# The rest of each weight slab made on VectorE, in a float32 transformer pair of blocks

## The reference, cut to what matters

```python
# block 1
proj = rmsnorm(x, attn_norm_g) @ w_in            # 1024 x 2312
x = x + concat(window_attention, forgetting_attention) @ w_out
x = x + square(relu(rmsnorm(x, mlp_norm_g) @ w_up)) @ w_down     # 1024 -> 4096 -> 1024
# block 2; the six mod vectors are silu(c) @ w_mod + b_mod (1024 x 6144)
h  = rmsnorm(x, g_pre_mix) * (1 + scale) + shift
x = x + gate * rmsnorm(concat(pool_mixer, neighbourhood_attention) @ w_out_2, g_post_mix)
x = x + gate2 * rmsnorm(square(relu(h2 @ w_mlp_in)) @ w_mlp_out, g_post_mlp)
```

## Time and profile before

| | us |
|---|---|
| three timed runs | 1270.38, 1274.62, 1275.14; median 1274.62 |
| the profiled execution, its own time | 1270.3 |
| its span, first to last instruction | 1268.4 |
| TensorE busy | 1208.7 (95%) |
| VectorE busy | 610.9 (48%) |
| ScalarE busy | 464.6 (37%) |
| GpSimd busy | 450.8 (36%) |

### The profile page before, as it was taken

The page is one execution under the profiler, slowest core; times in us unless marked ns, Lnnn a source line. Parts: engine busy times, 40 slices in busy tenths (PEclk is TensorE's granted clock), DMA queues, the critical chain, the costliest instruction groups (busy, mean ns, idle before and its releaser), DMA issues.

```text
span 1268.4 us, 16854 instructions
## 1 busy us (share of the span) xinstructions
PE 1208.7 (95%) x6252; PEld 998.0 (79%) x6252; DVE 610.9 (48%) x907; ACT 464.6 (37%) x828; POOL 450.8 (36%) x188
## 2 busy tenths in 40 slices
PE   5799999998999999999899999999899999999997
PEld 4677877787788788788779887778788888888885
DVE  5555445658767768651657223884721111111115
ACT  5455433425324334234342111432463251341441
POOL 3422220204444453463336320400255435353440
PEclk9999999999999999999889999999999999999999
DMA  7422120206665766643424311202243324233211
GB/s 228 116 85 67 62 87 2 85 17 216 233 215 191 241 211 210 227 134 132 133 67 143 99 67 26 67 2 83 67 140 108 119 67 132 67 105 94 83 50 66
DMA packets 75562, 144.10 MB, mean 114 GB/s; under 512 B 7234, under 2 KB 10050, under 8 KB 75490
## 3 DMA queue, kind: packets, MB, share of 16 engines
q1 hardware_dynamic: 53730, 98.46, 24.7%
q10 hardware_dynamic: 21760, 44.67, 10.6%
HBM read 140.20 MB, written 2.13 MB: 112 GB/s over the span
## 4 chain that ended last, share of the span: by engine, by line
PE 54%; issue 22%; DVE 11%; POOL 8%; ACT 2%; DMA 1%; ACTq 0%; POOLq 0%; DVEq 0%
PE gemm L950 16%; PE gemm L952 16%; PE gemm L951 16%; POOL w_lo L513 8%; DVE nmax L1860 1%; PE aux L1404 1%; DVE prob_t L1674 1%; DVE gemm L1859 1%; PE aux L991 1%; DVE xr L1465 1%; DVE xr L1460 1%; ACT junk L576 1%; DVE xt_lo L1471 1%; DMA mlp_gain<-in_g_pre_mlp 1%; PE gemm L1088 1%
## 5 line engine op out<-in xcount | busy, mean ns | idle before, releaser
L513 POOL TENSOR_TENSOR w_lo<-w_raw,w_hi 128x1024 fp32r<-128x1024 f32 (+1 forms) x180 | 445.7, 2498 | 780.2 <-ACT w_hi L741 422.3
L950 PE MATMUL gemm<-xt_hi,w_hi 128*128 128x512 f32 (+1 forms) x704 | 255.9, 363 | 5.0 <-issue 4.6
L951 PE MATMUL gemm<-xt_lo,w_hi 128*128 128x512 f32 (+1 forms) x704 | 254.8, 362 | 0.0
L952 PE MATMUL gemm<-xt_hi,w_lo 128*128 128x512 f32 (+1 forms) x704 | 254.5, 362 | 0.0
L950 PE MATMUL gemm<-w_hi,ht_hi 128*128 128x512 f32 x512 | 201.4, 393 | 3.8 <-POOL w_lo L513 3.8
L951 PE MATMUL gemm<-w_lo,ht_hi 128*128 128x512 f32 x512 | 200.0, 391 | 0.0
L952 PE MATMUL gemm<-w_hi,ht_lo 128*128 128x512 f32 x512 | 199.7, 390 | 0.0
L741 ACT ACTIVATE w_hi<-w_raw 128x1024 fp32r<-128x1024 f32 x124 | 125.7, 1050 | 175.6 <-PE gemm L952 130.0
L950 PEld LDWEIGHTS gemm<-xt_hi,w_hi 128*128 128x128 f32 x704 | 134.0, 190 | 27.1 <-issue 6.0
L1699 DVE TENSOR_TENSOR ht_lo<-hid,ht_hi 128x512 fp32r<-128x512 f32 x64 | 53.0, 828 | 210.7 <-ACT hid L754 210.7
L951 PEld LDWEIGHTS gemm<-xt_lo,w_hi 128*128 128x128 f32 x704 | 133.9, 190 | 20.2
(11 more groups left out here) (218 smaller groups left out, 1487.0 us busy)
## 6 DMA issues: line engine op xcount, KB each, us to landing
wm<-in_w_mod ACTq DMA_DIRECT2D x64, 512.0 KB, 4.8
w_raw<-in_w_in SPq DMA_DIRECT2D x32, 512.0 KB, 3.8
w_raw<-in_w_up SPq DMA_DIRECT2D x32, 512.0 KB, 4.0
w_raw<-in_w_down SPq DMA_DIRECT2D x32, 512.0 KB, 4.1
w_raw<-in_w_mlp_in SPq DMA_DIRECT2D x32, 512.0 KB, 4.2
w_raw<-in_w_mlp_out SPq DMA_DIRECT2D x32, 512.0 KB, 3.7
w_raw<-in_w_out SPq DMA_DIRECT2D x16, 512.0 KB, 3.7
x<-in_x SPq DMA_DIRECT2D x4, 512.0 KB, 7.7
```

The lines of the kernel that those rows point to most:

```text
L513: pool.tensor_tensor(w_lo[s % 2][:, ks, 0:width], raw[q][:, :, 0:width], w_hi[s % 2][:, ks, 0:width].bitcast(F32), ALU.subtract).then_inc( ...
L950: pe.matmul(bank, lh, rh, start=(k == 0), stop=False)
L951: pe.matmul(bank, lh, rl, start=False, stop=False)
L952: mm = pe.matmul(bank, ll, rh, start=False, stop=(k == KT - 1))
```

## The change

GpSimd no longer makes any w_lo; it keeps the four subtractions of the pooled rows. VectorE gets `low(s, q)`, the same subtraction on the same shapes with the same two semaphores, called at places written out by hand:

- slab 0: two units after the `scaled` of token tiles 1 and 2 of norm 1;
- slabs 1 and 2: two units ahead of `head_means(g)` for g = 0, 1 and 4, 5;
- slabs 3 to 7: one unit at the end of the half that follows the one in which ScalarE rounded it;
- both MLPs: of the next slab all four units at c = 0, of the one after two units each at c = 4 and 5, and of the two that follow (the second down slab and the next chunk's first up slab) one or two units each at c = 8, 9, 10, 12, 13 and 14;
- block 2: four units in a row after the last chunk, after the pool mixer's tiles, after the q tiles and after the k_c tiles; the second slab of w_out_2 one unit each in steps 5, 7, 9 and 11 of the neighbourhood attention; and four units ahead of tile 6 of w_out_2.

On ScalarE one thing moves: the units 4 to 7 of a chunk are rounded two at a time, before the ReLUs of tiles 4 and 5, where they were one each before tiles 4 to 7.

```diff
--- before.py
+++ after.py
@@ -64,7 +64,7 @@
 TILE_MLP2 = TILE_OUT2 + 2 * TT
 
 OUT2_ORDER = ((0, 0), (1, 0), (0, 1), (1, 1), (0, 2), (0, 3), (1, 2), (1, 3))
-POOL_SPLIT_IN = (13, 15, 17, 19)
+POOL_SPLIT_IN = (13,)
 SPLIT_IN_ATTENTION = (4, 6, 8, 10)
 
 
@@ -506,34 +506,10 @@
 
         @block_fn(nc, ctx, "gpsimd")
         def _(pool):
-            def low(s, q, width, wait):
-
-                pool.wait_ge(hi_split, wait)
-                ks = slice(UK * q, UK * (q + 1))
-                pool.tensor_tensor(w_lo[s % 2][:, ks, 0:width], raw[q][:, :, 0:width],
-                                   w_hi[s % 2][:, ks, 0:width].bitcast(F32), ALU.subtract).then_inc(unit_split, 1)
-
-            def lows(first, slabs):
-
-                with pool.Fori(0, slabs // 2) as i:
-                    for a in range(2):
-                        for q in range(UQ):
-                            low(first + a, q, NC, i * 8 + (4 * (first + a) + q + 1))
-                if slabs % 2:
-                    for q in range(UQ):
-                        low(first + slabs - 1, q, NC, 4 * (first + slabs - 1) + q + 1)
-
-            for s in range(N_IN1 + 1):
-                for q in range(UQ):
-                    low(s, q, KV_W if s == 1 else NC, 4 * s + q + 1)
-            lows(SLAB_OUT1 + 1, SLAB_OUT2 - SLAB_OUT1)
-            for q in range(UQ):
-                low(SLAB_OUT2 + 1, q, NC, 4 * (SLAB_OUT2 + 1) + q + 1)
             pool.wait_ge(pool_hi, 1)
             for j in range(4):
                 pool.tensor_tensor(xt_lo[:, j, :], pooled[:, j, :], xt_hi[:, j, :].bitcast(F32),
                                    ALU.subtract).then_inc(pool_lo, 1)
-            lows(SLAB_MLP2, SLABS - SLAB_MLP2)
 
 
         @block_fn(nc, ctx, "scalar")
@@ -757,8 +733,9 @@
                     for c in range(4):
                         split(c, i)
                     for c in range(8):
-                        if c >= 4:
-                            split(c, i)
+                        if c in (4, 5):
+                            split(2 * c - 4, i)
+                            split(2 * c - 3, i)
                         squared_relu(c, i)
                         if mod:
                             modulation(16 * i + c)
@@ -1473,10 +1450,21 @@
                                           token_cols(hi, half, cols, permute).bitcast(F32), ALU.subtract), xt_lo_done)
 
 
+            def low(s, q, i=0):
+
+                width = KV_W if s == 1 else NC
+                ks = slice(UK * q, UK * (q + 1))
+                dve.wait_ge(hi_split, i * 16 + (4 * s + q + 1))
+                dve.tensor_tensor(w_lo[s % 2][:, ks, 0:width], raw[q][:, :, 0:width],
+                                  w_hi[s % 2][:, ks, 0:width].bitcast(F32), ALU.subtract).then_inc(unit_split, 1)
+
             dve.wait_ge(gain1_loaded, 16)
             for m in range(TT):
                 stat(STAT_N1 + m)
                 scaled(NT_1 + m, STAT_N1 + m, x[:, m, :], gain1[:])
+                if m in (1, 2):
+                    low(0, 2 * m - 2)
+                    low(0, 2 * m - 1)
                 if m:
                     xt_low(NT_1 + m - 1, m - 1)
             xt_low(NT_1 + 3, 3)
@@ -1538,6 +1526,9 @@
                                           hst[:, 3, :].unsqueeze(2).broadcast_to([P, NH, HD]), ALU.mult), gemm_free)
 
             for g in range(PHASE):
+                if g % 4 < 2:
+                    low(g // 4 + 1, 2 * (g % 4))
+                    low(g // 4 + 1, 2 * (g % 4) + 1)
                 head_means(g)
                 head_rows(g)
 
@@ -1662,6 +1653,8 @@
                     xt_low(NT_2 + m, m, halves=[half])
                 for kind, n in halves_of(MIX_TURN, h):
                     mix_low(kind, n)
+                if h - 1 in SPLIT1:
+                    low(*SPLIT1[h - 1])
 
             mean_square(STAT_N2 + 3, STAT_N2 + 4)
             norm2_rows(3)
@@ -1685,13 +1678,20 @@
                                       aux[2 + b % 2][:].rearrange("p (h d) -> p h d", d=HD),
                                       rden[:, cols].unsqueeze(2).broadcast_to([P, NH, HD]), ALU.mult), heads_out)
 
-            def mlp(t0, acc, up0, mod, after, fresh=False):
+            def mlp(s0, t0, acc, up0, mod, after, fresh=False):
 
                 f0 = freed(t0 - 1)
 
                 def chunk(i, mod, after, fresh=False):
+
+                    def lows(*cs):
+                        for e in cs:
+                            if not isinstance(i, int) or 4 * i + s0 + e // 4 + 1 < SLABS:
+                                low(s0 + e // 4 + 1, e % 4, i)
+
                     for c in range(16):
                         bank = gp[(t0 + c) % 4]
+                        lows(*{0: (0, 1, 2, 3), 4: (4, 5), 5: (6, 7), 8: (8,), 12: (12,)}.get(c, ()))
                         if c < 8:
 
                             dve.wait_ge(hid_hi, i * 8 + (up0 + c + 1))
@@ -1707,6 +1707,8 @@
                                 dve.tensor_copy(cols, bank[:]).then_inc(gemm_free, 1)
                             else:
                                 dve.tensor_tensor(cols, cols, bank[:], ALU.add).then_inc(gemm_free, 1)
+                            if c % 4 < 3:
+                                lows(c + 1)
                             if after is not None:
                                 dve.wait_ge(gemm_free, i * 8 + (f0 + c - 7))
                                 after(c)
@@ -1791,7 +1793,9 @@
 
             did(dve.tensor_copy(ctmp[:, 0, :], csil[:, 0, :]), wm_used)
             modulation(-1)
-            mlp(TILE_MLP1, x, 0, True, norms_of_block_2)
+            mlp(SLAB_MLP1, TILE_MLP1, x, 0, True, norms_of_block_2)
+            for q in range(UQ):
+                low(SLAB_IN2 + 1, q)
             xt_low(NT_3 + 3, 3, True)
 
 
@@ -1817,10 +1821,14 @@
                                              upad[:, 8:8 + S], ALU.mult, ALU.subtract), pool_done)
                 g += 1
             assert tally.n[pool_step.name] == POOL_STEPS
+            for q in range(UQ):
+                low(SLAB_IN2 + 2, q)
             for j in range(4):
                 dve.wait_ge(gemm_done, g + 1)
                 did(dve.tensor_scalar(q_2[:, j, :], gp[g % 4][:], QSCALE, None, ALU.mult), gemm_free)
                 g += 1
+            for q in range(UQ):
+                low(SLAB_IN2 + 3, q)
             for j in range(4):
                 dve.wait_ge(gemm_done, g + 1)
                 did(dve.tensor_copy(k_2[:, j, :], gp[g % 4][:]), gemm_free)
@@ -1829,6 +1837,8 @@
                 dve.wait_ge(gemm_done, g + 1)
                 did(dve.tensor_copy(k_c[:, j, :], gp[g % 4][:, 0:CTX]), gemm_free)
                 g += 1
+            for q in range(UQ):
+                low(SLAB_OUT2, q)
             for j in range(4):
                 dve.wait_ge(pool_mixed, j + 1)
                 did(dve.tensor_scalar(pooled[:, j, :], aux[j][:], pscale[:, j:j + 1], None, ALU.mult), pool_scaled)
@@ -1872,6 +1882,8 @@
                         dve.wait_ge(turn_hi, 2 * TT + k + 1)
                         did(dve.tensor_tensor(grid_cols(xt_lo, k), grid_bank(aux[w % 2]),
                                               grid_cols(xt_hi, k).bitcast(F32), ALU.subtract), turn_read)
+                if i - 1 in SPLIT_IN_ATTENTION:
+                    low(SLAB_OUT2 + 1, SPLIT_IN_ATTENTION.index(i - 1))
 
 
             dve.wait_ge(tail_loaded, 16 * 5)
@@ -1884,6 +1896,9 @@
                 cols = slice(j * NC, (j + 1) * NC)
                 if e == 5:
                     xt_low(NT_4, 0)
+                if e == 6:
+                    for q in range(UQ):
+                        low(SLAB_MLP2, q)
                 dve.wait_ge(gemm_done, g + 1)
 
                 dve.wait_ge(ssq_done, tail_squares(e))
@@ -1922,7 +1937,7 @@
                     did(dve.scalar_tensor_tensor(x[:, m, cols], sub[:, m, cols], st[:, 3, k:k + 1], x[:, m, cols],
                                                  ALU.mult, ALU.add), fin_step)
 
-            mlp(TILE_MLP2, sub, 8 * NCH, False, last_norm, fresh=True)
+            mlp(SLAB_MLP2, TILE_MLP2, sub, 8 * NCH, False, last_norm, fresh=True)
 
 
 SILU_STEPS = 3 + 5 + 4
```

## The result

The changed kernel took 1267.49 us (median of four runs, 1266.03 to 1267.79), the kernel before in the same session 1274.63 (1270.38 to 1275.14). The ratio is 0.9941, with a 95% interval of 0.9923 to 0.9960: a gain of 7.1 us, where 17.3 were forecast.

What follows compares the result with a forecast made beforehand. TensorE was taken as the bound, busy 1208.7 of 1268.4 us, with waits on GpSimd's w_lo and on VectorE standing still behind GpSimd. Stage terms summed to -17.3, from the median 1274.6 to 1257.3 us; range 1247 to 1272.

Steps and rivals of the forecast that it cites:

- its own signs of being wrong: Mod steps over 1 us, new TensorE waits over 1 us for hid_lo, a maximum or w_lo, or changed full-clock busy time.
- Opening, heads (0 and -1.5): 0 to 66 us: opening unchanged; in the heads TensorE's waits for qn shrink, -0.8 for the first, -0.7 for two others.
- First attention (+1): 20 subtractions, 24.6 us of VectorE, placed between maxima and copies, hardly delay TensorE: +1, bounds 0 and 24.6.
- Start of the first MLP (-5.2): Mod steps finish sooner, the 3.6 us wait for mod_lo goes, and 1.6 us of clock returns: -5.2.
- Rest of the first MLP (-3.8): Three waits for w_lo at c = 8 go because the slab's fourth unit is finished by tile 6: -3.8.
- Norms of block 2 (-8): Waits shrink by 3.2 and 2.1, the clock returns 4.2, a late xt_lo costs 1.5: -8, bounds -2 and -10.
- w_out_2 and second MLP (-2.4): A 2.5 us wait behind VectorE's standstills goes; the second MLP has nothing to give: -2.4.
- Neighbourhood attention (+2.6): Four subtractions in the loop of VectorE and TensorE each cost 0.64 us beyond idle time: +2.6, bounds 0 and 5.
- The level: The profiled execution took 1270.3 us; the forecast sum was instead set on the runs' median, 1274.6 us.
- the gain comes in part: Rival: norms, start of the MLP and attention fall short as new gaps replace old: -4.1, 1270.5 us; chance 0.15.
- VectorE as the bound: Rival: in the first MLP mod steps stay at 1.18 us and VectorE falls behind TensorE: 1289 us; chance 0.06.
- The new places collide: Rival: each of 24 subtractions in the attentions delays TensorE in full: +9, 1284 us; chance 0.05.

Runs made afterwards that it cites:

- run 3: Changed kernel with VectorE's four subtractions of slab 6 moved from halves 33 to 36 to halves 38 to 41 of the first attention: 1261.96 us, ratio 0.9876.
- run 2: Changed kernel with VectorE's four subtractions of slab 7 moved from halves 55 to 58 to halves 65 to 68 of the first attention: 1259.58 us, ratio 0.9880.
- runs 7 and 8: Changed kernel with w_mod's loads ahead of tile 0 of the first MLP, 1258.85 us; or its four opening subtractions behind tile 0's ht_lo, 1262.05 us.
- run 14: Kernel before, all subtractions still on GpSimd, with only ScalarE's regrouping of units 4 to 7: 1267.37 us, ratio 0.9938.
- run 5: Changed kernel with the four subtractions of w_out_2's second slab back on GpSimd, the other 176 on VectorE: 1259.39 us, ratio 0.9876.
- Run 1: The kernel before, unchanged, measured again in ten runs: median 1275.77 us.

## Why the prediction was half right, point by point

The direction, the prices of the instructions and every removed standstill were right. The forecast fell short at three terms of its sum, by 8.5, 7.4 and 3.8 us (the other terms came out 4.6 better than forecast), and one gain had another cause than it named. Of its own signs of being wrong one came: new waits of over 1 us behind a maximum (1.37 at 258.9, 1.59 at 804.9).

- **Opening, heads (0 and -1.5): -3.2 together.** The first wait for qn fell from 4.2 to 3.3, as I took it; the half-clock stretch of 3.4 us at 65 went too, which was not counted (luck, in part: four profiles of later kernels with the same opening show one near 62).
- **First attention (+1): +9.5. This step failed.** "I am near 0" was argued from the earlier trace rows, from the waits that were there, and not from the slack that VectorE had at each of the 20 places. (The rows stop at 3.6 us; just below them stood 1.8 us for prob_ta, also in this stage.) Three of the five slabs cost nothing. At the other two TensorE waited: slab 6 cost 2.3 us of waits (run 3: 1.9), and at slab 7, where VectorE had 2.7 us of idle time from 241 to 252 and got three subtractions, 3.7, the price was under 1 us of waits and 6 of clock (run 2: 7.9 in all).
- **Start of the first MLP (-5.2): +2.2. This step failed.** The mod steps did finish their first three in 2.4 us and the subtractions took 4.6. "After which the next steps come" did not ask what they read: w_mod was issued at 300.06 into a burst of w_raw transfers that the fast subtractions had set free, and VectorE idled 5.0 us. A transfer took the place of the standstill (runs 7 and 8). Here the skipped question was what is late next.
- **Rest of the first MLP (-3.8): -5.0**, the size near, the cause half right. "I cost it at nothing by itself", of ScalarE's regrouping, failed: it took all three waits away without VectorE (run 14, 3.8 us of waits), 8.2 us with what the clock gave back.
- **Norms of block 2 (-8): -8.4.** The chain had 1.23 for mod_scale, the wait of 3.9 shrank to 0.5, the two half-clock stretches of 6.8 us went, and the last xt_lo came 1.5 us late, all as forecast.
- **Projections (0): 0**, and **w_out_2 and second MLP (-2.4): -3.7.**
- **Neighbourhood attention (+2.6): +6.4.** The mechanism was right: three waits of 0.76 where 0.20 were, 0.56 each against 0.64 forecast. The fourth subtraction fell together with the end of a pair's row, where TensorE waited 1.59 instead of 0.46 us. The waits add up to 2.8; what the term left out is the clock, some 3.6 us (run 5: 2.4 of waits, 5.1 of clock).
- **The level.** The sum was made against an execution of 1270.3 and set on the median of 1274.6, as if their difference were a constant. Run 1 shows that it was 4 us of clock.

The rivals: "the gain comes in part", 1270.5, came nearest to the first session, and its reason, new gaps in the place of the old ones, is what happened, though not in the norms. Its premise, that a stretch follows any gap, does not hold: the waits of 1.87 us at 512.8 and 2.54 at 905.9 in the kernel before have none behind them. VectorE as the bound is out: a mod step takes 750 ns. The rule of the Trainium skill's page "Vector Engine (DVE) Microarchitecture Reference", section "Points that are easy to get wrong", that a scalar_tensor_tensor with two SBUF sources that are not bf16 runs at half throughput, is not borne out here either: 112 steps of 512 columns with two float32 sources in SBUF took 750 ns, the subtractions ht_lo of the same size, also with two, 692. "The new places collide" had the mechanism right and the price wrong: the four places in the neighbourhood attention and those of two of five slabs in the first collided, not all, and most of the price was the clock's, which that rival did not count.

What stays open: what decides, at the same waits, whether the clock falls and for how long. The runs show chances only.
